# Second feed-forward product and the residual's last token tile with GpSimd at rest

## Chip, cores, metric

One core of one Trainium2 chip runs the whole layer as one program. The metric is the device time of a run in microseconds (us). TensorE multiplies, VectorE and GpSimd do element-wise work, ScalarE copies and activates, SyncE (SP) issues all DMAs.

## What is computed

One layer of a diffusion backbone over 1024 latent tokens of width 1024 with 256 context tokens. Three mixer branches are merged, added to `x`, and followed by a SwiGLU feed-forward with sandwich RMSNorm. What matters here is its end, float32 throughout:

```python
x = x + mod_x[2] * rms_norm(mix, norm_g[l, 1])
h2 = modulate(x, norm_g[l, 2], mod_x[3], mod_x[4])
x = x + mod_x[5] * rms_norm(swiglu(h2, w_ffn_in[l], w_ffn_out[l]), norm_g[l, 3])
# swiglu: gate, up = split(h @ w_in); (silu(gate) * up) @ w_out     D_FF = 2816
```

## The kernel before, in words

**High and low parts.** Each float32 operand of a matmul is cut in two: the high part is a ScalarE copy into the fp32r type, the low part is the operand minus the high part, by VectorE or GpSimd. `parts_product` (L74) issues three matmuls, high by high (L78), high by low (L79) and low by high (L80), of 128x512 each.

**Seven products.** The feed-forward matrices are multiplied with a two-by-two scheme of seven products for eight (Winograd's), P1 to P7. It needs sums and differences of tiles, made by VectorE in SBUF, each of which is cut again.

**residual_ffn_in** (L2012) first makes the output projection of the mixer, one token tile t of 128 rows after the other (0 to `LAST` = 7), adds it to `x`, normalises the rows, turns them on TensorE (L2188) and modulates them into `h2`. Then it runs over 22 pairs of weight tiles (pair p, gate and up), with seven products of 12 matmuls each. Pair 0 begins before the last token tile is done, in the order 0, 3, (0 of pair 1), 1, 2, 4, 6, 5. For it VectorE and GpSimd make the parts of the turned operands while the rows of tile 7 are still on the way:

- VectorE's loop over t ends for t = 7 with the copy of product 0 from PSUM to `t1` (L2614), which product 3 waits for; then it writes `h2` for half the rows, two sums (L2649, L2651), three `part_lower` (L2551), `second_sum` (L2554), the far low parts of T2 (L2661), `fourth_sum` (L2558), the low parts of T4 and `z` (L2680), then the sums for pair 1 (`s13` L2569/L2571, `s2`, `s4`). Product 1 waits for the seventh `part_lo`.
- GpSimd makes sums (L2463, L2466, L2518, L2523, L2527), low parts of weights (`first_weight_lo` L2473 for two tiles of pair 0; `weight_lo` L2477 for later pairs), the near low part of T2 and the four of B22 (`t_part_lo` L2481). Then it makes only `weight_lo` in the loop over the pairs.
- ScalarE makes the high parts (`t1_hi`, `t3_hi`, `t_part_hi`, `weight_hi`), squares and SiLU.

**ffn_out** (L2891) is the second product. It has 7 x 11 = 77 steps s of 12 matmuls each, in the order P1, P5, P6, P3, P2, P7, P4. A step uses one slot of a ring of six with four parts: w high (L2860) and f high (L2862) on ScalarE, w low on VectorE (L2872), f low on GpSimd (`pool_cut`, L2867). VectorE also makes the sum of w tiles for a later product (`dve_sum`, L2886) in steps of P1, P5, P3 and P2. The raw tiles come by DMA (`sp_load`): f into four buffers, w into six, of which P1 and P3 take two a step (`W_LOADS`); a w buffer is free once its sum is made, an f buffer once its low part is (L2841 waits for it). The first steps are started inside the last pair of `residual_ffn_in` by `early[...]`: loads for steps 0 to 4, cuts and sums for steps 0 and 1. The sums of the last activation pair (`keep["last_sums"]`, L2720 to L2724) run in VectorE's step 6, their store (L2154) in SP's step 8.

TensorE waits for banks: `join` (L3036) adds a finished PSUM bank to rows in SBUF, after P3 (before P2 takes the banks), after P2, and after P7 (before P4 goes on in them). Of the first 512 rows, `lower` (VectorE, L3039) scales 128x1024 and GpSimd adds `x` (L3026); the store and the reload of `x` follow (L2921, L2922). The last 512 rows end with L3066, L3073, L3078 and the store L2925.

Each engine runs its own list in order, so the order of calls in a block is its schedule; all waits are semaphores.

Of the kernel before, what the change touches and what calls it, by code (L numbers as in the profile page):

```python
# [41 lines left out]
P = 128  # L42
# [1969 lines left out]
def residual_ffn_in(nc, sem, block, banks, io, keep):  # L2012
# [8 lines left out]
    with ExitStack() as ctx:  # L2021
# [57 lines left out]
        keep["f_stored"] = ((PRODUCT_STEPS - 1, keep["ffn"]["stored"][0]), (PRODUCT_STEPS, keep["ffn"]["stored"][2]),  # L2079
# [31 lines left out]
        def _(sp):  # L2111
# [52 lines left out]
            for p in (FC - 2, FC - 1):  # L2164
                if p == FC - 2:
                    sp.wait_ge(fw_lo_ready, (FC - 1) * PRODUCTS)
                    for s in range(3):
                        early["sp"](sp, s)
                if p == FC - 1:
                    for s in range(3, 5):  # L2170
                        early["sp"](sp, s)
# [101 lines left out]
        def _(act):  # L2273
# [96 lines left out]
            modulate(LAST - 1, 0, 5)  # L2370
            square_x(LAST)
# [78 lines left out]
        def _(pool):  # L2450
# [20 lines left out]
            def first_weight_lo(i):  # L2471
                pool.wait_ge(w0_hi, w0_at(i))
                pool.tensor_tensor(f_lo[i], source(0, i), f_hi[i].bitcast(F32), ALU.subtract).then_inc(w0_lo, 1)  # L2473

# [4 lines left out]
            def t_part_lo(n, ks, at, hi, done):  # L2479
                pool.wait_ge(t_hi_ready[n], hi)  # L2480
                pool.tensor_tensor(t_lo[:, n, ks, at], src[n][:, ks, at], t_hi[:, n, ks, at].bitcast(F32), ALU.subtract)\  # L2481
                    .then_inc(done, 1)

            def step(p, q):
                if q == FC - 1:
                    early["pool"](pool, 0)
                    early["pool"](pool, 1)
# [40 lines left out]
            for i in W0[3:]:  # L2528
                first_weight_lo(i)
            t_part_lo(T2, slice(0, KH), slice(0, HALF // 2), 1, t_lo_ready[T2])  # L2530
            for k in range(KH):
                t_part_lo(B22, k, slice(0, HALF), k // 2 + 1, t_lo_ready[B22])
# [5 lines left out]
        def _(v):  # L2538
# [17 lines left out]
            def fourth_sum(at, count):  # L2556
                v.wait_ge(t2_sum, count)
                v.tensor_tensor(src[T4][:, :, at], src[T4][:, :, at], src[T2][:, :, at], ALU.subtract).then_inc(t4_sum, 1)  # L2558

# [38 lines left out]
            for t in range(TL):  # L2598
# [13 lines left out]
                if t == LAST:  # L2612
                    v.wait_ge(prod0, prod0_at(0))
                    v.tensor_copy(t1, banks[0]).then_inc(t1_ready, 1)  # L2614
# [5 lines left out]
                v.tensor_scalar(xn[:], x[t % 2][:], root(1), None, ALU.mult).then_inc(xn_ready, 1)  # L2620
                if 1 <= t <= FH:
                    h_parts(t - 1)
                if t == LAST - 1:
# [4 lines left out]
                    for i in W0[:3]:  # L2628
                        v.wait_ge(w0_hi, w0_at(i))
                        v.tensor_tensor(f_lo[i], source(0, i), f_hi[i].bitcast(F32), ALU.subtract).then_inc(w0_lo, 1)  # L2630
# [31 lines left out]

# [587 lines left out]
```

## Time and profile before

| | us |
|---|---|
| runs before: median (lowest, highest) of 3 | 1833.17 (1830.52, 1833.98) |
| the profiled execution: its own time | 1832.09 |
| its span, first to last instruction | 1830.0 |
| TensorE busy (matmul) | 1762.9 (96%) |
| VectorE busy | 1236.0 (68%) |
| ScalarE busy | 801.9 (44%) |
| GpSimd busy | 886.6 (48%) |

A matmul's busy time is modelled and overlaps its neighbour's, so the distance between starts tells TensorE's pace, and gaps tell its waits. "Idle before" is time in which the engine stood before an instruction, and the name behind it is what ended the wait. The second product runs from 1596 us to the end, the last token tile of the residual from about 1155 to 1205 us.

### The profile page before, as it was taken

How to read it: one execution, taken by the hardware profiler on the slowest of the kernel's cores; microseconds unless marked ns; L12 is line 12 of the kernel's file. 1: busy time of each engine (PE TensorE's matmuls, PEld its weight loads, DVE VectorE, ACT ScalarE, POOL GpSimd, SP SyncE). 2: the span in 40 equal slices, each digit the busy share in tenths (PEclk: the TensorE clock that was granted, in tenths of full speed). 3: DMA queues.
4: the chain of work that ended last, by engine and by line, in shares of the span. 5: the costliest groups of instructions: out<-in, count | busy, mean ns of one | idle time of the engine just before them, and what ended most of it. 6: DMA issues, size and time to landing. Idle time of an engine off the chain costs nothing.

```text
span 1830.0 us, 25729 instructions
## 1 busy us (share of the span) xinstructions
PE 1762.9 (96%) x9180; PEld 1489.0 (81%) x9180; DVE 1236.0 (68%) x1634; ACT 801.9 (44%) x1579; POOL 886.6 (48%) x550
## 2 busy tenths in 40 slices
PE   8999999999989999899999999899999999989997
PEld 6997888888878888798988878678888888878785
DVE  3528688889949888577743366875565665675866
ACT  3434333335537777555520145543333333344453
POOL 0307677775526967320022242665555555454564
PEclk9999999999999999999999999899999999999998
DMA  8333234336585665411034242123224232376624
GB/s 314 107 106 132 93 149 166 123 138 235 217 204 149 153 159 143 107 32 70 1 138 155 88 161 88 74 93 126 92 103 138 92 126 92 135 264 209 235 89 167
DMA packets 98375, 249.86 MB, mean 137 GB/s; under 512 B 12257, under 2 KB 25953, under 8 KB 98146
## 3 DMA queue, kind: packets, MB, share of 16 engines
q1 hardware_dynamic: 98274, 248.52, 40.7%
q8 instruction: 63, 1.03, 0.2%
q14 instruction: 38, 0.31, 0.1%
HBM read 183.07 MB, written 65.41 MB: 136 GB/s over the span
## 4 chain that ended last, share of the span: by engine, by line
PE 81%; DVE 9%; ACT 3%; DMA 2%; issue 2%; SPq 1%; POOL 1%; PEldq 0%; DVEq 0%; ACTq 0%; POOLq 0%
PE psum L78 19%; PE psum L79 18%; PE psum L80 18%; PE psum L106 3%; PE psum L109 3%; PE psum L107 3%; PE psum L1251 3%; PE psum L1589 2%; PE psum L1238 2%; PE psum L1239 2%; PE psum L1246 1%; PE psum L1575 1%; DVE wmx L1777 1%; DVE mx L1345 1%; PE psum L409 1%
## 5 line engine op out<-in xcount | busy, mean ns | idle before, releaser
L729 POOL TENSOR_TENSOR ring<-raw_w,ring 128x512 fp32r<-128x512 f32 x120 | 187.3, 1579 | 137.5 <-ACT ring L600 137.5
L78 PE MATMUL psum<-h_hi,ring 128*128 128x512 f32 x400 | 155.9, 390 | 3.3 <-ACT z L646 2.0
L79 PE MATMUL psum<-h_lo,ring 128*128 128x512 f32 x400 | 155.6, 389 | 0.0
L80 PE MATMUL psum<-h_hi,ring 128*128 128x512 f32 x400 | 155.6, 389 | 0.0
L78 PE MATMUL psum<-u_slot 128*128 128x512 f32 x308 | 122.4, 398 | 11.8 <-DVE u_high L3036 5.6
L80 PE MATMUL psum<-u_slot 128*128 128x512 f32 x308 | 121.8, 395 | 0.0
L79 PE MATMUL psum<-u_slot 128*128 128x512 f32 x308 | 121.6, 395 | 0.0
L600 ACT ACTIVATE ring<-raw_w 128x512 fp32r<-128x512 f32 x120 | 72.5, 625 | 98.9 <-DVE raw_w L889 31.7
L1286 ACT ACTIVATE e<-psum,neg_m 128x1280 f32<-128x1280 f32 x64 | 85.1, 1330 | 43.5 <-DVE neg_m L1346 43.5
L1345 DVE TENSOR_REDUCE mx<-psum 128x1 f32<-128x1280 f32 x64 | 95.1, 1486 | 5.7 <-PE psum L1239 3.1
L2477 POOL TENSOR_TENSOR cut_lo<-i_raw,cut_hi 128x512 fp32r<-128x512 f32 x44 | 66.8, 1520 | 59.3 <-ACT cut_hi L2331 59.3
L78 PEld LDWEIGHTS psum<-h_hi,ring 128*128 128x128 f32 x400 | 75.1, 188 | 19.9 <-issue 3.4
L2477 POOL TENSOR_TENSOR cut_lo<-stage,cut_hi 128x512 fp32r<-128x512 f32 x40 | 59.9, 1499 | 64.0 <-ACT cut_hi L2331 64.0
L80 PEld LDWEIGHTS psum<-h_hi,ring 128*128 128x128 f32 x400 | 75.1, 188 | 15.8
L79 PEld LDWEIGHTS psum<-h_lo,ring 128*128 128x128 f32 x400 | 75.1, 188 | 15.4
L2867 POOL TENSOR_TENSOR u_slot<-u_f,u_slot 128x512 fp32r<-128x512 f32 x39 | 55.4, 1423 | 59.1 <-ACT u_slot L2862 59.1
L78 PEld LDWEIGHTS psum<-u_slot 128*128 128x128 f32 x308 | 59.0, 192 | 25.9 <-DVE u_slot L2872 7.8
L2867 POOL TENSOR_TENSOR u_slot<-h,u_slot 128x512 fp32r<-128x512 f32 x38 | 55.5, 1466 | 48.5 <-ACT u_slot L2862 48.5
L1251 PE MATMUL psum<-val,at 128*128 128x128 f32 x640 | 76.9, 275 | 1.1 <-ACT at L1293 1.1
L1671 ACT ACTIVATE we<-psum,wneg_m 128x640 f32<-128x640 f32 (+1 forms) x64 | 49.1, 768 | 65.8 <-DVE wneg_m L1779 63.0
L1238 PE MATMUL psum<-k_st,q_st 128*128 128x512 f32 (+1 forms) x192 | 72.4, 384 | 4.9 <-ACT e L1286 3.9
L78 PE MATMUL psum<-m_parts,i_hi 128*128 128x512 f32 x176 | 70.5, 401 | 5.4 <-issue 5.1
(410 smaller groups left out, 5405.7 us busy)
## 6 DMA issues: line engine op xcount, KB each, us to landing
raw_w<-in_w_pairs SPq DMA_DIRECT2D x40, 512.0 KB, 4.8
qk_dram<-room SPq DMA_DIRECT2D x26, 512.0 KB, 3.6
room<-in_w_ada SPq DMA_DIRECT2D x24, 512.0 KB, 4.9
gates_dram<-ost SPq DMA_DIRECT2D x24, 512.0 KB, 3.1
b_g<-gates_dram SPq DMA_DIRECT2D x8, 1536.0 KB, 7.7
stage<-in_w_ff SPq DMA_DIRECT2D x22, 512.0 KB, 5.9
i_raw<-in_w_ff SPq DMA_DIRECT2D x22, 512.0 KB, 5.0
f_dram<-h SPq DMA_DIRECT2D x22, 512.0 KB, 3.1
```

Of the source, the lines that this page charges most:

```text
L78: pe.matmul(out, sh, mh, start=first, stop=False, skip_group_check=onto)
L79: pe.matmul(out, sh, ml, start=False, stop=False, skip_group_check=onto)
L80: return pe.matmul(out, sl, mh, start=False, stop=last, skip_group_check=onto)
L106: pe.matmul(out, sh, mh, start=first, stop=False)
L600: act.activation(w_hi[i], source(p, i), ACT.Copy).then_inc(w_hi_ready, 1)
L729: pool.tensor_tensor(w_lo[i], source(p, i), w_hi[i].bitcast(F32), ALU.subtract).then_inc(w_lo_ready, 1)
L1238: pe.matmul(out, q, k_st[j][:, s, c0:c0 + w], start=True, stop=False)
L1251: mm = pe.matmul(bank[:, 2 * P:3 * P], at[t % 2][:, k, :], val[t // TL % 2][:, k, :], start=(k == 0), stop=(k == TT - 1))
L1286: act.activation(e[i % 2][s][:], psum[:, 3 * s * HALF:3 * s * HALF + TOK], ACT.Exp, scale=SCALE, bias=neg_m[:, i % 2, s:s + 1], accum_out= ...
L1345: ch.link(v.tensor_reduce(mx[:, s:s + 1], psum[:, 3 * s * HALF:3 * s * HALF + TOK], AX.X, ALU.max))
L2477: pool.tensor_tensor(f_lo[i], source(q, i), f_hi[i].bitcast(F32), ALU.subtract).then_inc(fw_lo_ready, 1)
L2867: pool.tensor_tensor(slot[:, 3, :], keep["f_raw"][s % F_RAWS], slot[:, 2, :].bitcast(F32), ALU.subtract).then_inc(b["f_lo_sem"], 1)
```

## The change

- **Second product.** The low part of f moves from GpSimd to VectorE (`f_cut`), as does the last addition to the lower rows (`lower_out`), one `lower` or `lower_out` a step. GpSimd keeps only the f cuts of steps 0 and 1. The second w tile of P1 and P3 gets four buffers of its own (`seconds`), loaded from behind the last products on; the six others hold one main tile a step. Sums come two steps later (`SUM_LAG`), behind the join after P3. The last activation sums move from step 6 to 10, their store from step 8 to 14. The early loads grow to four and then two steps.
- **Residual, last token tile.** `t1` is copied by ScalarE. The low parts of weights 4 and 5 of pair 0, of T2's near half and of B22 move from GpSimd to VectorE; `fourth_sum` goes ahead of T2's low parts.

```diff
@@ -2076,7 +2076,7 @@
-        keep["f_stored"] = ((PRODUCT_STEPS - 1, keep["ffn"]["stored"][0]), (PRODUCT_STEPS, keep["ffn"]["stored"][2]),
+        keep["f_stored"] = ((PRODUCT_STEPS - 1, keep["ffn"]["stored"][0]), (PRODUCT_STEPS, (fs_out, 16 * (FC // 2 - 1))), (2 * PRODUCT_STEPS - 1, keep["ffn"]["stored"][2]),
@@ -2164,10 +2164,10 @@
-                    for s in range(3):
+                    for s in range(F_RAWS):
...
                 if p == FC - 1:
-                    for s in range(3, 5):
+                    for s in range(F_RAWS, F_RAWS + 2):
@@ -2368,6 +2368,9 @@
+            act.wait_ge(prod0, prod0_at(0))
+            act.wait_ge(taken, TL)
+            act.activation(t1, banks[0], ACT.Copy).then_inc(t1_ready, 1)
@@ -2468,23 +2471,14 @@
-            def first_weight_lo(i):
-                pool.wait_ge(w0_hi, w0_at(i))
-                pool.tensor_tensor(f_lo[i], source(0, i), f_hi[i].bitcast(F32), ALU.subtract).then_inc(w0_lo, 1)
...
-            def t_part_lo(n, ks, at, hi, done):
-                pool.wait_ge(t_hi_ready[n], hi)
-                pool.tensor_tensor(t_lo[:, n, ks, at], src[n][:, ks, at], t_hi[:, n, ks, at].bitcast(F32), ALU.subtract)\
-                    .then_inc(done, 1)
...
                 if q == FC - 1:
-                    early["pool"](pool, 0)
-                    early["pool"](pool, 1)
+                    early["f"](pool, 0)
+                    early["f"](pool, 1)
@@ -2525,11 +2519,6 @@
-            for i in W0[3:]:
-                first_weight_lo(i)
-            t_part_lo(T2, slice(0, KH), slice(0, HALF // 2), 1, t_lo_ready[T2])
-            for k in range(KH):
-                t_part_lo(B22, k, slice(0, HALF), k // 2 + 1, t_lo_ready[B22])
@@ -2556,6 +2545,10 @@
+            def first_weight_lo(i):
+                v.wait_ge(w0_hi, w0_at(i))
+                v.tensor_tensor(f_lo[i], source(0, i), f_hi[i].bitcast(F32), ALU.subtract).then_inc(w0_lo, 1)
@@ -2610,14 +2603,15 @@
                 if t == LAST:
-                    v.wait_ge(prod0, prod0_at(0))
-                    v.tensor_copy(t1, banks[0]).then_inc(t1_ready, 1)
+                    first_weight_lo(4)
...
+                if t == LAST:
+                    first_weight_lo(5)
@@ -2626,8 +2620,7 @@
                     for i in W0[:3]:
-                        v.wait_ge(w0_hi, w0_at(i))
-                        v.tensor_tensor(f_lo[i], source(0, i), f_hi[i].bitcast(F32), ALU.subtract).then_inc(w0_lo, 1)
+                        first_weight_lo(i)
@@ -2660,10 +2653,11 @@
+            v.wait_ge(t4_sum, 2)
+            fourth_sum(far, FH - 1)
+            t_part_lo(T2, slice(0, KH), slice(0, HALF // 2), 1, t_lo_ready[T2])
...
-            v.wait_ge(t4_sum, 2)
-            fourth_sum(far, FH - 1)
@@ -2728,10 +2722,8 @@
-                    early["sum"](v, 0)
...
-                    early["sum"](v, 1)
@@ -2750,6 +2742,8 @@
+            for k in range(KH):
+                t_part_lo(B22, k, slice(0, HALF), k // 2 + 1, t_lo_ready[B22])
@@ -2765,27 +2759,29 @@
-RING, F_RAWS, W_RAWS = 6, 4, 6
+RING, F_RAWS, W_RAWS, SECONDS = 6, 4, 6, 4
...
-W_LOADS = {P1: (("even", 0), ("even", 1)), P5: (("odd", 1),), P3: (("odd", 1), ("even", 1)), P2: (("odd", 0),)}
+W_MAIN = {P1: ("even", 0), P5: ("odd", 1), P3: ("odd", 1), P2: ("odd", 0)}
+W_SECOND = {P1: ("even", 1), P3: ("even", 1)}
...
-def loads_until(s):
+SUM_LAG = 2
+def load_of(table, s):
...
-    return sum(len(W_LOADS.get(n, ())) for n in range(i)) * PRODUCT_STEPS + j * len(W_LOADS.get(i, ()))
+    return sum(n in table for n in range(i)) * PRODUCT_STEPS + j
+def step_of(table, n):
+    return sorted(table)[n // PRODUCT_STEPS] * PRODUCT_STEPS + n % PRODUCT_STEPS
...
-def step_of_load(n):
-    return next(s for s in range(STEPS) if loads_until(s) <= n < loads_until(s + 1))
@@ -2802,10 +2798,11 @@
+        seconds = [sb(f"u_second{n}", [P, HALF])[:] for n in range(SECONDS)]
...
-    stage, w_in = keep["stage"], keep["u_in"]
+    stage, w_in, second_in = keep["stage"], keep["u_in"], [sem(f"fo_second{n}") for n in range(SECONDS)]
@@ -2820,19 +2817,32 @@
-        return other[:, j, :] if i == P7 else chain[j] if i in SUMS_OF else w_raw[loads_until(s) % W_RAWS]
-    def landed(eng, n):
+        return other[:, j, :] if i == P7 else chain[j] if i in SUMS_OF else w_raw[load_of(W_MAIN, s) % W_RAWS]
+    def landed(eng, s):
+        n = load_of(W_MAIN, s)
...
+    def rows_of(s, what):
+        rows, half = what
+        chunk = 2 * (s % PRODUCT_STEPS) + (rows == "odd")
+        return io["w_ffn_out"][chunk * P:(chunk + 1) * P, half * HALF:(half + 1) * HALF]
+    def sp_second(sp, s):
+        if s // PRODUCT_STEPS not in W_SECOND:
+            return
+        n = load_of(W_SECOND, s)
+        if n >= SECONDS:
+            sp.wait_ge(b["w_sum_sem"], sums_until(step_of(W_SECOND, n - SECONDS)))
+        sp.dma_start(seconds[n % SECONDS], rows_of(s, W_SECOND[s // PRODUCT_STEPS])).then_inc(second_in[n % SECONDS], 16)
...
-        for a, (rows, half) in enumerate(W_LOADS.get(i, ())):
-            n, chunk = loads_until(s) + a, 2 * j + (rows == "odd")
+        if i in W_MAIN:
+            n = load_of(W_MAIN, s)
             if n >= W_RAWS:
-                sp.wait_ge(b["w_sum_sem"], sums_until(step_of_load(n - W_RAWS)))
-            sp.dma_start(w_raw[n % W_RAWS], io["w_ffn_out"][chunk * P:(chunk + 1) * P, half * HALF:(half + 1) * HALF])\
-              .then_inc(w_in[n % W_RAWS], 16)
+                sp.wait_ge(b["w_sum_sem"], sums_until(step_of(W_MAIN, n - W_RAWS)))
+            sp.dma_start(w_raw[n % W_RAWS], rows_of(s, W_MAIN[i])).then_inc(w_in[n % W_RAWS], 16)
@@ -2854,17 +2864,17 @@
-            landed(act, loads_until(s))
+            landed(act, s)
...
-    def pool_cut(pool, s):
+    def f_cut(eng, s):
...
-        pool.wait_ge(b["f_hi_sem"], s + 1)
-        pool.tensor_tensor(slot[:, 3, :], keep["f_raw"][s % F_RAWS], slot[:, 2, :].bitcast(F32), ALU.subtract).then_inc(b["f_lo_sem"], 1)
+        eng.wait_ge(b["f_hi_sem"], s + 1)
+        eng.tensor_tensor(slot[:, 3, :], keep["f_raw"][s % F_RAWS], slot[:, 2, :].bitcast(F32), ALU.subtract).then_inc(b["f_lo_sem"], 1)
@@ -2875,17 +2885,19 @@
-        n = loads_until(s)
-        raws = [w_raw[(n + a) % W_RAWS] for a in range(len(W_LOADS[i]))]
-        for a in range(len(raws)):
-            landed(v, n + a)
+        landed(v, s)
+        main, second = w_raw[load_of(W_MAIN, s) % W_RAWS], None
+        if i in W_SECOND:
+            n = load_of(W_SECOND, s)
+            v.wait_ge(second_in[n % SECONDS], 16 * (n // SECONDS + 1))
+            second = seconds[n % SECONDS]
...
-        out, left, right = {P1: lambda: (chain[j], raws[1], raws[0]), P5: lambda: (chain[j], raws[0], chain[j]),
-                            P3: lambda: (other[:, j, :], raws[0], raws[1]), P2: lambda: (chain[j], raws[0], chain[j])}[i]()
+        out, left, right = {P1: (chain[j], second, main), P5: (chain[j], main, chain[j]),
+                            P3: (other[:, j, :], main, second), P2: (chain[j], main, chain[j])}[i]
...
-    keep["ffn_out"], keep["ffn_out_cuts"] = b, {"sp": sp_load, "act": act_cut, "pool": pool_cut, "dve": dve_cut, "sum": dve_sum}
+    keep["ffn_out"], keep["ffn_out_cuts"] = b, {"sp": sp_load, "act": act_cut, "f": f_cut, "dve": dve_cut, "sum": dve_sum, "second": sp_second}
@@ -2907,12 +2919,15 @@
     def _(sp):
-        for s in range(5, STEPS):
+        sp.wait_ge(*before["products"])
+        for s in range(SECONDS):
+            cuts["second"](sp, s)
+        for s in range(6, STEPS):
+            cuts["second"](sp, s - SUM_LAG)
...
-            if s == 8:
+            if s == 14:
...
             if s == 3 * PRODUCT_STEPS:
-                sp.wait_ge(*before["products"])
@@ -3015,16 +3030,6 @@
-    @block.gpsimd
-    def _(pool):
-        for s in range(2, STEPS):
-            cuts["pool"](pool, s)
-            t = s - (end_of(P2) + RING + 6)
-            if 0 <= t < T:
-                pool.wait_ge(y_ready, t + 1)
-                pool.wait_ge(x_in[t], 16)
-                nc.gpsimd.tensor_tensor(low[:, t, :], low[:, t, :], x[t][:], ALU.add).then_inc(out_ready, 1)
@@ -3039,13 +3044,22 @@
+        def lower_out(t):
+            v.wait_ge(y_ready, t + 1)
+            v.wait_ge(x_in[t], 16)
+            v.tensor_tensor(low[:, t, :], low[:, t, :], x[t][:], ALU.add).then_inc(out_ready, 1)
+        LOWER = {5: (lower, 0), 6: (lower_out, 0), 7: (lower, 1), 8: (lower_out, 1), 9: (lower, 2), 11: (lower_out, 2),
+                 12: (lower, 3), 13: (lower_out, 3)}
+        v.wait_ge(b["f_lo_sem"], 2)
...
-            cuts["sum"](v, s)
-            if s == 6:
-                keep["last_sums"]()
+            cuts["f"](v, s)
             if s == end_of(P3) + RING - 1:
                 join(P3, Y, low, right)
+            cuts["sum"](v, s - SUM_LAG)
+            if s == 10:
+                keep["last_sums"]()
@@ -3055,8 +3069,9 @@
-            if 0 <= s - (end_of(P2) + RING + 5) < 4:
-                lower(s - (end_of(P2) + RING + 5))
+            if s - end_of(P2) - RING in LOWER:
+                finish, t = LOWER[s - end_of(P2) - RING]
+                finish(t)
```

## Rows read from the trace of the kernel before

**Rows 1.** Waits of TensorE, 1560 to 1831 us: total, times, longest.

```profile
PE psum L78 <- DVE u_high L3036: 5.6, 1, 5.6
PE psum L78 <- POOL u_slot L2867: 3.7, 1, 3.7
PE psum L78 <- DVE u_slot L2872: 1.4, 1, 1.4
PE psum L78 <- DVE u_low L3036: 1.2, 1, 1.2
```

**Rows 2.** Tile u_slot: ns min/median/max, first and last start.

```profile
L78 PE MATMUL psum<-u_slot x308: 387/389/766, 1596.2 to 1823.1; 128*128 128x512 f32 x154
...
L2872 DVE TENSOR_TENSOR u_slot<-stage,u_slot x22: 675/692/1757, 1586.2 to 1735.0; 128x512 fp32r<-128x512 f32 x22
```

**Rows 3.** Timeline of TensorE: start, duration, what; quiet stretch.

```profile
1639.66 0.39 PE L80 MATMUL psum<-u_slot 128*128 128x512 f32 x1
...
1719.94 0.39 PE L79 MATMUL psum<-u_slot 128*128 128x512 f32 x1
```

**Rows 4.** Busy by stretch: length, PE, PEld, DVE, ACT, POOL, granted clock, DMA.

```profile
1620.00:1630.00 10.00, 6.32 (x21) 4.80 (x20) 5.66 (x6) 5.34 (x9) 4.40 (x3) 0.75 0.96 341
```

**Rows 5.** Chain that ended last: start, us, what.

```profile
1627.03 0.43 PE psum L79
```

**Rows 6.** Timelines of VectorE and GpSimd in the second product.

```profile
1597.93 1.79 DVE L2708 TENSOR_TENSOR h<-i_g,i_z 128x512 f32<-128x512 f32 x1
...
1723.29 1.78 DVE L2886 TENSOR_TENSOR u_chain<-u_first,u_chain 128x512 f32<-128x512 f32 x1
...
1784.28 2.31 DVE L3039 SCALAR_TENSOR_TENSOR u_low<-u_low,u_ss,late_row 128x1024 f32<-128x1024 f32 x1
...
1723.24 1.28 POOL L2867 TENSOR_TENSOR u_slot<-u_f,u_slot 128x512 fp32r<-128x512 f32 x1 [1.44 <-ACT u_slot L2862]
```

**Rows 7.** Tile u_high: ns min/median/max, first and last start.

```profile
L2982 ACT ACTIVATE u_high<-psum x4: 578/591/604, 1665.7 to 1667.2; 128x512 f32<-128x512 f32 x4
L3036 DVE TENSOR_TENSOR u_high<-psum,u_high x4: 673/674/677, 1790.9 to 1792.7; 128x512 f32<-128x512 f32 x4
...
L3078 DVE SCALAR_TENSOR_TENSOR u_high<-u_high,u_ss,u_x x4: 1284/1286/1286, 1817.5 to 1825.7; 128x1024 f32<-128x1024 f32 x4
```

**Rows 8.** Timeline of SP, the DMA issues.

```profile
1615.14 0.55 SPq L2154 DMA_DIRECT2D fs_dram<-h  x1
1615.73 1.69 SPq L2834 DMA_DIRECT2D stage<-in_w_ffn_out  x2
```

**Rows 9.** DMA issues of 1598 to 1603 us: size, median us to landing.

```profile
u_first<-in_w_ffn_out SPq DMA_DIRECT2D x2, 256.0 KB, 3.0
```

**Rows 10.** DMA issues of 1585 to 1640 us.

```profile
stage<-in_w_ffn_out SPq DMA_DIRECT2D x17, 256.0 KB, 5.1
```

**Rows 11.** Timeline of TensorE at the last token tile: [idle before <- releaser].

```profile
1162.70 0.50 PE L78 MATMUL psum<-b_hi,cut_hi 128*128 128x512 f32 x1 [2.96 <-DVE gate_row L2614]
...
1176.54 0.77 PE L78 MATMUL psum<-m_parts,i_hi 128*128 128x512 f32 x1 [5.09 <-issue]
```

**Rows 12.** Timelines at the last token tile: ScalarE, GpSimd, VectorE.

```profile
1159.41 1.83 ACT L2298 ACTIVATE h<-psum,B,A 128x128 f32<-128x128 f32 x5
...
1172.50 2.79 POOL L2481 TENSOR_TENSOR i_t_lo<-h,i_t_hi 128x1024 fp32r<-128x1024 f32 x1
...
1169.78 1.64 DVE L2649 TENSOR_TENSOR h<-h 128x512 f32<-128x512 f32 x1 [0.17 <-ACT h L2298]
...
1173.01 4.03 DVE L2551 TENSOR_TENSOR m_parts<-h,m_parts 128x512 fp32r<-128x512 f32 x3
1176.96 1.21 DVE L2554 TENSOR_TENSOR h<-h 128x1024 f32<-128x1024 f32 x1
...
1187.93 1.77 DVE L2569 TENSOR_TENSOR i_s<-i_raw 128x512 f32<-128x512 f32 x1
...
1205.41 0.69 DVE L2680 TENSOR_TENSOR i_z<-i_z,psum 128x512 f32<-128x512 f32 x1 [1.33 <-ACT i_z L2393]
```

## Prediction

> **What bounds the kernel now.** I read the waits of TensorE first. In the last 270 us it stops four times, for 1.4, 3.7, 1.2 and 5.6 us, 11.9 us in all, each time for a low part or a join on VectorE or GpSimd [rows 1]. The rest of the second feed-forward product is TensorE alone. Its 308 first matmuls start from 1596.2 to 1823.1 us [rows 2]. The undisturbed pitch comes from a quiet stretch: 354 matmuls start from 1639.66 to 1719.94 us, so 80.28 / 353 = 0.2274 us each [rows 3]. A step is 12 matmuls, 2.73 us, and 307 groups of three would take 209.4 us; they take 226.9. The stage loses 17.5 us. 11.9 are the four waits. The other 5.6 come from the clock: after the 3.7 us stop the granted clock of the slice is 0.75, between its two levels of 1.2 and 2.4 GHz [rows 4], and the matmuls stand 0.43 us apart [rows 5]. The first restart has 12 such pitches and the second 8, which is 20 x 0.20 = 4.0 us, and 1.6 us go into the uneven first matmuls after the four stops.
>
> Why is VectorE late, when its low part takes 0.69 us at the median [rows 2]? The timeline shows it. At 1723.24 GpSimd begins a 1.28 us cut, at 1723.29 VectorE a sum, and the sum ends 0.55 us after GpSimd: 1.78 us instead of 0.69 [rows 6]. A 128x1024 product of three operands in SBUF takes 2.31 us beside GpSimd [rows 6] and 1.29 us without it [rows 7]. So the two engines take turns on such operands. That, and not the amount of work, makes the four stops.
>
> **Start of the product.** Before, the weights of a step share six buffers, two for each step of the first eleven, so the queue waits for VectorE's sums, which stand behind the last activation product. The load behind the 3.7 us stop was issued at 1615.73, right behind the store of sums at 1615.14 that had waited for VectorE [rows 8]. After: a main tile for each of six steps and four f tiles are loaded early, the sums come two steps later, the store moves from step 8 to step 14. Everything that VectorE does in a step is then low part of w, low part of f, sum: 3 x 0.69 = 2.07 us [rows 2] against 2.73 us. GpSimd's 75 cuts of this block are gone. So the first two stops (1.4, 3.7) and the first slow clock stretch vanish, if nothing else is late.
>
> What is late next is the new second tile. Its load stands behind the wait for the last products (over by 1596.2) and the f store, which waits for VectorE's last product. That took 1.79 us from 1597.93 beside GpSimd [rows 6] and would take 0.69, so 1598.6. Issue of the store, 0.55 us as at 1615.14 [rows 8], puts the second tile's at 1599.2. VectorE makes the parts of step 2 by 1600.0 and then stands at the sum of step 0, with the parts of step 3, the next sum and all f loads from step 6 on behind it. TensorE wants step 3 at 1596.2 + 3 x 2.73 = 1604.4. The nearest landing, of the loads issued just here before, is 3.0 us [rows 9]: 1602.2. Sum, w part, f part: 2.07 us, 1604.3. Loss about 0. The far row is the 5.1 us median of the crowded stretch [rows 10]: 1604.3 + 2.07 = 1606.4, loss 2.0 us. I take 0.3, since one 512 KB store is ahead, as it was for the loads of [rows 9]. The Trainium skill (DMA: Bandwidth & Descriptors, Anatomy of one DMA) gives a fixed 2.0 us plus bytes over 436 GB/s; as an estimate, 2.6 us for 256 KB, by which the loss would be 0. The trace lies above it, at 3.0 and 5.1.
>
> Behind that, VectorE's 2.07 us a step lets it gain on TensorE. The loads are the same in number and size as before, only earlier; I cost them at nothing. What hides them is VectorE's lead of up to five steps (the ring); without it each would cost what it lands late, at most the 5.1 us of [rows 10].
>
> **Joins and residual rows.** The join of P3 now comes before the sum. In the old order the sum of 1.78 us stood ahead of it [rows 6]; now a 0.69 us f part does. The w part ends as the sum began, at 1723.3, the f part by 1724.0, the first join of 0.67 us [rows 7] by 1724.7. Before, it ended at 1723.29 + 1.78 + 0.67 = 1725.7, and TensorE had waited 1.2, so it wants the bank at 1724.5. The 1.2 us stop shrinks to 0.2. The rows' two passes over `low` (2.31 us on VectorE, more on GpSimd) cost VectorE now 1.29 + 1.29 us a tile, one pass a step: 2 x 0.69 + 1.29 = 2.67 us, still under 2.73, with the six-slot ring (five steps, 13.6 us) as cover. So the join of P7 should not be late: 5.6 us become 0.2, and the second clock stretch goes. If the cover were gone, what remains is 4 x 1.29 us.
>
> Sum for this block: 17.5 lost before, 0.3 + 0.2 + 0.2 after and 0.3 for restarts: 1.0. **Gain 16.5 us.** Bounds: 14 (the far landing, half a restart) and 17.5.
>
> **The residual's last tile.** TensorE's large waits here are 3.0 us for the copy of t1 and 5.1 us, shown as issue [rows 11]. The copy moves to ScalarE, which is free at 1161.24 [rows 12] and needs 0.59 us [rows 7]: TensorE goes on at 1161.9, not 1162.7 [rows 11]. That is not kept. VectorE's low part 4 takes the copy's place, meets GpSimd and delays the row mean by up to 0.5 us. With it go xn, ScalarE's next parts and GpSimd's first low part of the next pair, for which TensorE waits next. I take 0.3 us later there, between 0 and 0.6.
>
> The 5.1 us stop that ends at 1176.5 is VectorE's chain: two sums of 1.64 us and three parts in 4.03 us, beside GpSimd's low parts, of which one runs 2.79 us from 1172.50 [rows 12]. With GpSimd done by about 1170, that is one op of about 1.3 and four of 0.69: 4.1 us instead of 7.3, and the seventh part, the one TensorE needs, ends at 1172.8 rather than 1176.5. TensorE itself is ready at 1171.5 (1176.54 - 5.09), so the stop shrinks to 1.3.
>
> Then VectorE has more to do: the near T2 part (1.29), four B22 parts (4 x 0.69) which were GpSimd's. The chain ran 1176.96 to 1187.93 before its first sum for the next pair, with ScalarE and TensorE between. I walk it: second sum 1174.5, fourth sum 1175.9, T2 parts 1178.5, T4 and z by 1181.8, B22 by 1184.4. The next pair's first sum took 1.77 us at 1187.93 beside GpSimd [rows 12], 0.69 when alone, 1.1 us more. Gain 3.5 + 1.1 = 4.6 us. From here the chain is VectorE's to the z of pair 1 at 1205.41 [rows 12], after which TensorE waits no more, so what VectorE gains there is kept; slow clock saved at 1177 is absorbed in this chain. **Gain 4.6 us**, bounds 1.5 (rival C) and 7 (also the slow clock).
>
> **Sum.** 16.5 + 4.6 = 21.1 us off the profiled 1832.1 is 1811.0. The median of the runs is 1.1 us above the profiled one: 1812.1. I give 1812.
>
> **Rivals.**
> A, slower: the turn-taking is not what stretches VectorE; its ops stay at the means they have in this block. Low parts are then about 0.98 us and sums 1.2. Against 0.91 (a third of 2.73), the point from which it decides, a step with a sum takes 3.16 us: 44 such steps x 0.43 = 19 us lost, with the two join stops (6.8) and 3 us of clock kept: 1812 + 29 = 1841. For it: VectorE takes 75 cuts and 4 row passes more. Against: pairs as at 1723 [rows 6], and a 0.69 median [rows 2]. 4%. The Trainium skill (SBUF — State Buffer, SBUF: two separate sides) has one exclusive pair of ports for the two engines, held for a whole instruction; the trace agrees, with 0.55 us behind the end of GpSimd's cut [rows 6].
> B: the second tile lands late, 6.7 us or so. TensorE stops 3.6 us at step 3 and gets half clock as it did at 1626 (2.7 us): 1818. For it: VectorE is in order and everything stands behind the sum. Against: the queue is empty but for one store. 12%.
> C: the residual's gain is lost, because VectorE has 5 us more work in a chain that was its own: only the 1.1 us and a little remain, 1815. 14%.
> D: VectorE's row passes and the squares' wait reach into the P7 join; half of the stop and a clock stretch stay: 1816 to 1818. 6%.
> E: the change does not do what it says, since GpSimd keeps the sums and weight parts of the residual and the pairs and is at rest only in the last block: the residual gives nothing, 1816. 3%, for the block itself keeps its gain.
>
> **Numbers.** Forecast 61%, A 4, B 12, C 14, D 6, E 3. The bounds of the terms give 1808 to 1817; with B, C, D and E the range is 1808 to 1820, which leaves out A and little else. A measurement can tell 0.2%, 3.7 us, from no change: faster 94%, same 2%, slower 4%.
>
> **What would show it.** No GpSimd work after the first two cuts; VectorE's u_slot and u_chain ops all at 0.69 us; TensorE's waits in the last block together under 1.5 us and granted clock 1.00 in all its full slices; ScalarE, not VectorE, writing t1; the stop at 1176 near 1.3 us and starting product 1 at about 1173; the second product's first to last matmul in about 210.5 us. The forecast is wrong if a stop over 2 us with half clock stands near step 3, if a join is waited for, or if the residual chain to the z of pair 1 ends less than 3 us earlier.

## The result, and the profile after

| | before | after |
|---|---|---|
| runs: median (lowest, highest), us | 1831.92 (1830.52, 1833.98) of 4 | 1812.52 (1808.0, 1820.69) of 4 |
| ratio, 95% interval | | 0.9885 [0.9856, 0.9913] |
| the profiled execution, us | 1832.09 | 1820.69 |
| its span, us | 1830.0 | 1818.9 |

The change saves 1.15%, 19.4 us between the medians; the forecast was 1812.0, in a range of 1808 to 1820. A second series of five rounds gave a ratio of 0.9879 [0.9852, 0.9906] (`after_again`, below); in it one run of the kernel before, in a slow state, took 3553.69 us and is left out of the medians.

The two profiled executions are only 11.4 us apart. The missing part lies ahead of the changed code, where both kernels are the same. Here is the busy time by stretch of the attention stage, columns as in [rows 4]; first the kernel after:

```profile
720.00:760.00 40.00, 35.58 (x236) 31.70 (x235) 20.94 (x35) 22.49 (x56) 20.97 (x17) 0.89 0.37 118
760.00:800.00 40.00, 38.81 (x254) 36.36 (x255) 22.90 (x71) 20.38 (x47) 11.05 (x6) 0.86 0.31 71
```

and the kernel before:

```profile
720.00:760.00 40.00, 35.58 (x270) 31.70 (x269) 22.32 (x43) 22.69 (x56) 20.97 (x17) 1.00 0.40 127
760.00:800.00 40.00, 38.34 (x291) 35.55 (x290) 28.27 (x85) 23.89 (x56) 13.35 (x8) 1.00 0.29 66
```

In 80 us the kernel after makes 71 matmuls fewer (236 + 254 against 270 + 291) at a granted clock of 0.89 and 0.86: an episode in which the clock is partly at its lower level. Kernels that are the same up to here had it in some executions and not in others: `block_only` and `gpsimd_keeps_f` (both 0.89 in the second of these slices) did, `rest_only` and `t_parts_gpsimd` (1.00 in both) did not. So I measure stages, not totals. The last matmul ahead of the stop for `t1` starts at 1159.35 before and at 1169.63 after, 10.28 us later. From there:

| stretch, us | before | after | gain |
|---|---|---|---|
| residual: last matmul ahead of the `t1` stop, to the restart behind `z` of pair 1 | 1159.35 to 1206.24: 46.89 | 1169.63 to 1210.84: 41.21 | 5.7 |
| from there to the first matmul of the second product | 389.96 | 389.96 | 0.0 |
| second product, first to last start of the 308 | 1596.2 to 1823.1: 226.9 | 1600.8 to 1812.1: 211.3 | 15.6 |
| last of the 308 to the end of the span | 6.9 | 6.8 | 0.1 |

5.7 + 15.6 + 0.1 = 21.4 us, less the 10.3 of the episode is 11.1, the difference of the spans.

**Second product.** The engines' busy time from the page, GpSimd's by slice, and all waits of TensorE from 1560 to 1820 us in the kernel after:

```profile
PE 1765.8 (97%) x9180; PEld 1493.8 (82%) x9180; DVE 1228.2 (68%) x1719; ACT 801.0 (44%) x1580; POOL 754.2 (41%) x464
...
POOL 0307677775525967330012232445555555400000
```

```profile
PE psum L78 <- DVE u_slot L2877: 0.7, 1, 0.7
```

GpSimd is silent in the last five slices. Of the four waits of [rows 1], 11.9 us together, one of 0.7 is left. VectorE has 86 instructions of GpSimd's more across the program (550 - 464), and yet is busy for 8 us less than the 1236.0 of before. The tile u_slot and the windows say why:

```profile
L2877 DVE TENSOR_TENSOR u_slot<-h,u_slot x38: 680/684/693, 1603.6 to 1795.0; 128x512 fp32r<-128x512 f32 x38
...
L2882 DVE TENSOR_TENSOR u_slot<-u_first,u_slot x23: 680/692/694, 1610.2 to 1777.7; 128x512 fp32r<-128x512 f32 x23
L2882 DVE TENSOR_TENSOR u_slot<-stage,u_slot x22: 681/692/693, 1590.8 to 1736.8; 128x512 fp32r<-128x512 f32 x22
```

```profile
1600.00:1640.00 40.00, 39.27 (x173) 32.11 (x172) 31.65 (x51) 18.26 (x33) 0.00 (x0) 1.00 0.82 282
...
1760.00:1800.00 40.00, 39.91 (x176) 32.66 (x175) 32.53 (x48) 22.29 (x42) 0.00 (x0) 1.00 0.46 158
```

VectorE's slowest cut is 694 ns, where [rows 2] had 1757, and the clock is 1.00 where [rows 4] had 0.75. The wait that is left comes from the second w tile (`u_second`). It shows in the timelines of SP and VectorE and the DMA issues of 1600 to 1610 us:

```profile
1603.12 0.55 SPq L2173 DMA_DIRECT2D f_dram<-h  x1
1603.70 5.17 SPq L2837 DMA_DIRECT2D u_second<-in_w_ffn_out  x5
...
1607.82 0.69 DVE L2898 TENSOR_TENSOR u_first<-u_second,stage 128x512 f32<-128x512 f32 x1 [3.53 <-issue]
1608.43 0.69 DVE L2882 TENSOR_TENSOR u_slot<-stage,u_slot 128x512 fp32r<-128x512 f32 x1
1609.03 0.68 DVE L2877 TENSOR_TENSOR u_slot<-h,u_slot 128x512 fp32r<-128x512 f32 x1
```

```profile
u_second<-in_w_ffn_out SPq DMA_DIRECT2D x5, 256.0 KB, 4.1
```

Issued at 1603.70, landed by 1607.82, and the low part of f, third from there, ends at 1609.71: TensorE goes on at 1609.87. In the kernel before, the first loads of [rows 9] were issued farther behind the same store, 2.53 us and not 0.58:

```profile
1599.74 0.55 SPq L2173 DMA_DIRECT2D f_dram<-h  x1
1602.27 0.80 SPq L2834 DMA_DIRECT2D u_first<-in_w_ffn_out  x2
```

**Residual.** TensorE's timeline at the last token tile (to compare with [rows 11], take off 10.28):

```profile
1169.63 0.39 PE L80 MATMUL psum<-b_hi,cut_lo 128*128 128x512 f32 x1
1172.07 0.50 PE L78 MATMUL psum<-b_hi,cut_hi 128*128 128x512 f32 x1 [2.05 <-ACT gate_row L2373]
...
1179.21 0.50 PE L78 MATMUL psum<-b_hi,cut_hi 128*128 128x512 f32 x1 [2.30 <-POOL cut_lo L2476]
...
1182.99 0.47 PE L78 MATMUL psum<-m_parts,i_hi 128*128 128x512 f32 x1 [0.72 <-issue]
...
1210.84 0.47 PE L78 MATMUL psum<-i_t_hi,cut_hi 128*128 128x512 f32 x1 [1.30 <-POOL i_lo L2476]
```

The 5.09 us stop is 0.72. Before, six matmuls from 1164.59 and ten from 1177.11 stood 0.43 us apart, at a granted clock of 0.50, behind the stops of 2.96 and 5.09; now none does. What TensorE gains by that in the first of the two stretches it gives up in a wait: the one that ends at 1179.21 is 2.30 us and was 0.22. The timelines of VectorE and GpSimd:

```profile
1172.26 1.78 DVE L2551 TENSOR_TENSOR cut_lo<-stage,cut_hi 128x512 fp32r<-128x512 f32 x1
...
1183.40 1.22 DVE L2543 TENSOR_TENSOR h<-h 128x1024 f32<-128x1024 f32 x1
1184.73 1.23 DVE L2547 TENSOR_TENSOR h<-h 128x1024 f32<-128x1024 f32 x1
1185.87 3.63 DVE L2654 TENSOR_TENSOR i_t_lo<-h,i_t_hi 128x1024 fp32r<-128x1024 f32 x5
1189.41 0.68 DVE L2674 TENSOR_TENSOR i_z<-i_z,psum 128x512 f32<-128x512 f32 x1
1190.01 3.69 DVE L2654 TENSOR_TENSOR i_t_lo<-h,i_t_hi 128x512 fp32r<-128x512 f32 x6
1193.62 0.69 DVE L2562 TENSOR_TENSOR i_s<-i_raw 128x512 f32<-128x512 f32 x1
...
1195.78 1.29 POOL L2476 TENSOR_TENSOR i_lo<-i_raw,i_hi 128x512 fp32r<-128x512 f32 x1 [15.38 <-ACT i_hi L2331]
```

GpSimd is idle for 15.38 us, and VectorE goes through ten low parts of 128x512 and one of 128x1024 in 7.3 us. It starts the first sum of pair 1 at 1193.62. Counted from the last matmul ahead of the stop, as all stages here, that is 1183.34 on the clock of before, 4.6 us ahead of its 1187.93, and the sum takes 0.69 rather than 1.77 [rows 12].

### The profile page after: what moved, and what is told of

It reads as the page before. It is cut to its first block and busy times, and to the rows that moved or that the text cites. A ratio compares the mean times of both kernels' runs of the same rounds, so it can differ in the third digit from the quotient of the medians.

```text
span 1818.9 us, 25732 instructions
## 1 busy us (share of the span) xinstructions
PE 1765.8 (97%) x9180; PEld 1493.8 (82%) x9180; DVE 1228.2 (68%) x1719; ACT 801.0 (44%) x1580; POOL 754.2 (41%) x464
## 5 line engine op out<-in xcount | busy, mean ns | idle before, releaser
L78 PE MATMUL psum<-u_slot 128*128 128x512 f32 x308 | 120.4, 391 | 0.9 <-DVE u_slot L2877 0.7
L80 PE MATMUL psum<-u_slot 128*128 128x512 f32 x308 | 120.1, 390 | 0.0
L79 PE MATMUL psum<-u_slot 128*128 128x512 f32 x308 | 119.9, 389 | 0.0
L78 PEld LDWEIGHTS psum<-h_hi,ring 128*128 128x128 f32 x400 | 75.1, 188 | 19.4 <-issue 3.4
L79 PEld LDWEIGHTS psum<-h_lo,ring 128*128 128x128 f32 x400 | 75.1, 188 | 15.3
L1251 PEld LDWEIGHTS psum<-val,at 128*128 128x128 f32 x640 | 75.9, 196 | 1.8 <-ACT at L1293 1.0
L78 PE MATMUL psum<-b_hi,cut_hi 128*128 128x512 f32 x176 | 69.0, 392 | 5.1 <-POOL cut_lo L2476 2.3
L78 PE MATMUL psum<-i_t_hi,cut_hi 128*128 128x512 f32 x176 | 68.6, 390 | 1.3 <-POOL i_lo L2476 1.3
```

Of the source, the lines that this page charges most:

```text
L78: pe.matmul(out, sh, mh, start=first, stop=False, skip_group_check=onto)
L79: pe.matmul(out, sh, ml, start=False, stop=False, skip_group_check=onto)
L80: return pe.matmul(out, sl, mh, start=False, stop=last, skip_group_check=onto)
L1251: mm = pe.matmul(bank[:, 2 * P:3 * P], at[t % 2][:, k, :], val[t // TL % 2][:, k, :], start=(k == 0), stop=(k == TT - 1))
```

## The experiments

The theory: VectorE and GpSimd take turns on operands in SBUF, and GpSimd's rest, not the new buffers, gives most of the gain. Each run is read by the two stage times, residual (46.9 before, 41.2 after) and second product (226.9 and 211.3), from one profiled execution each.

**One part alone.** `block_only` keeps `residual_ffn_in`'s last tile as it was, and `residual_only` keeps the second product as it was:

```diff
 # block_only
-            act.activation(t1, banks[0], ACT.Copy).then_inc(t1_ready, 1)
+            for i in W0[3:]:
+                first_weight_lo(i)          # on GpSimd, and t_part_lo of T2 and B22 too
 # residual_only
-RING, F_RAWS, W_RAWS, SECONDS = 6, 4, 6, 4
+RING, F_RAWS, W_RAWS = 6, 4, 6
```

> The change in the second product alone, the residual's last tile as before. If the two parts are separate, as the working has it, the first to last of the 308 first matmuls of the second product take 211.3 us as in the changed kernel (226.9 before), TensorE waits 3.0 and 5.1 us again at the last tile, and the time is 15.6 us below before. If part of the block's gain hung on the earlier arrival from the residual, the block would take 213 us or more.

> The change at the residual's last tile alone, the second product as before. Separate parts: the block takes 226.9 us, and from TensorE's last matmul before the t1 wait to its restart behind the z of pair 1 there are 41.2 us instead of 46.9, so 5.7 us below before. If the residual's gain is only a loan that later pairs take back, the second product starts less than 3 us earlier.

Measured: `block_only` 46.97 and 211.6, `residual_only` 41.22 and 226.5. The two parts add without touching each other: 15.3 and 5.7 us.

**GpSimd's rest alone.** The second product with the buffers, loads, sums and stores of before, but `pool_cut` and the lower rows' addition called from VectorE's list, and the join of P3 where it was. The passes over the lower rows are spread one a step, as in the changed kernel:

```diff
         for s in range(2, STEPS):
             cuts["dve"](v, s)
+            cuts["pool"](v, s)
             cuts["sum"](v, s)
```

> Second product: VectorE makes the f low parts and the last additions, GpSimd rests; but loads, buffers, the place of the sums and of the store stay as before, residual as before. Turn-taking theory: all VectorE ops are at 0.69 us, the first two stops all but vanish because the sums and the store come earlier by themselves, the P3 join waits under 1 us since the sum of 0.69 us is ahead of it, the P7 join not at all: block 210.5 to 213 us. Load-order theory (the gain is from the new buffers, the later sums and the later store): the 3.7 us stop and its clock stretch stay, block 217 us or more.

**GpSimd not at rest.** The changed kernel, with the f cuts and the addition left on GpSimd, and VectorE's four passes in four steps in a row, as before:

```diff
+    @block.gpsimd
+    def _(pool):
+        for s in range(2, STEPS):
+            cuts["f"](pool, s)
...
-            cuts["f"](v, s)
```

> The changed kernel with new buffers, load order, late sums and store, but the f low parts from step 2 on and the last additions on GpSimd. Turn-taking theory: VectorE's ops that meet GpSimd take 1.6 to 1.8 us again, the passes over the lower rows 2.3; the P7 join waits 3 us or more with half clock behind it, block 217 to 222 us. Load-order theory: the block is within 1 us of the changed kernel's 211.3.

Measured: second product 212.7 in `rest_only` (1598.1 to 1810.8) and 220.8 in `gpsimd_keeps_f` (1598.2 to 1819.0). The waits of TensorE in `rest_only`:

```profile
PE psum L78 <- DVE u_slot L2867: 1.5, 1, 1.5
PE psum L78 <- DVE u_low L3026: 0.7, 1, 0.7
```

and in `gpsimd_keeps_f`, with VectorE's and GpSimd's timelines around the long one:

```profile
PE psum L78 <- DVE u_high L3051: 5.6, 1, 5.6
PE psum L78 <- DVE u_slot L2882: 1.7, 2, 1.3
```

```profile
1774.22 2.32 DVE L3054 SCALAR_TENSOR_TENSOR u_low<-u_low,u_ss,late_row 128x1024 f32<-128x1024 f32 x1
1776.46 2.88 DVE L2882 TENSOR_TENSOR u_slot<-u_first,u_slot 128x512 fp32r<-128x512 f32 x1
...
1785.92 2.47 DVE L3051 TENSOR_TENSOR u_high<-psum,u_high 128x512 f32<-128x512 f32 x4
...
1785.41 2.81 POOL L3041 TENSOR_TENSOR u_low<-u_low,u_x 128x1024 f32<-128x1024 f32 x1
```

With the arrangement of before, the rest alone gives 14.2 of the 15.6 us, in spite of 79 instructions more on VectorE. The spread of the passes is in these 14.2; no run has the one without the other. The new arrangement without the rest gives 6.1 (226.9 - 220.8): the 3.7 us stop and the wait at the join of P3 are gone and two short waits of 1.7 us together are left, but the join of P7 waits 5.6 us as in [rows 1]. There VectorE's 0.69 us cut takes 2.88 and its 1.29 us pass 2.32, beside GpSimd's cuts and additions. The join itself, four operations with one operand in PSUM, is not stretched, though it runs beside an addition of GpSimd's: it takes 2.47 us, one operation every 0.60 us. On top of the rest the arrangement is worth 1.4.

**Is it the turn-taking, or the work?** Two kernels give GpSimd work whose result nobody reads, beside the changed kernel's second product. `extra_tt` adds 75 subtractions of 128x512 from SBUF, `extra_memset` 150 fills of 128x512:

```diff
+        for s in range(2, STEPS):
+            pool.wait_ge(b["f_hi_sem"], s + 1)
...
+            pool.tensor_tensor(b["extra"], spare[:, 0:HALF], spare[:, HALF:D], ALU.subtract)   # extra_tt
+            pool.memset(b["extra"], 0.0)                                        # extra_memset, twice
```

> The changed kernel, and beside each step of the second product one GpSimd subtraction of 128x512 float32 from SBUF whose result nobody reads; VectorE's work is as in the changed kernel. Turn-taking theory: VectorE's three ops a step meet it, those met take 1.3 to 1.8 us, a summed step costs VectorE about 2.07 + 1.1 = 3.2 us against 2.73, so the block grows from 211.3 to 225 us or more. If GpSimd only did harm through results that came late, the block stays at 211.3 since nobody waits for it.

> The same with two GpSimd fills of 128x512 with zero a step, which read nothing from SBUF. If any GpSimd access takes the turn, VectorE's ops stretch as in the run with subtractions. If only a GpSimd op that reads SBUF does, they stay at 0.69 us and the block at 211.3. The Trainium skill (SBUF — State Buffer, SBUF: two separate sides) says the second for VectorE ops with two SBUF inputs.

Measured: residual 41.2 in both, second product 244.6 with the subtractions and 211.3 with the fills. The 308 first matmuls and the busy time by stretch, `extra_tt`:

```profile
L78 PE MATMUL psum<-u_slot x308: 387/389/765, 1591.1 to 1835.7; 128*128 128x512 f32 x154
...
1600.00:1640.00 40.00, 34.63 (x144) 27.97 (x145) 39.93 (x47) 17.87 (x31) 21.47 (x12) 0.96 0.79 262
```

`extra_memset`:

```profile
L78 PE MATMUL psum<-u_slot x308: 389/389/473, 1588.0 to 1799.3; 128*128 128x512 f32 x154
L2883 DVE TENSOR_TENSOR u_slot<-stage,u_slot x22: 684/693/696, 1578.0 to 1724.1; 128x512 fp32r<-128x512 f32 x22
...
1600.00:1640.00 40.00, 40.00 (x178) 32.98 (x177) 35.77 (x58) 22.79 (x40) 18.29 (x35) 1.00 0.87 296
```

GpSimd is busy for 21.5 and 18.3 of 40 us, much the same, but VectorE makes 47 instructions in 39.9 us of busy time in the one and 58 in 35.8 in the other. Timelines of `extra_tt`:

```profile
1719.37 1.77 DVE L2899 TENSOR_TENSOR u_other<-stage,u_second 128x512 f32<-128x512 f32 x1
...
1718.88 1.71 POOL L3042 TENSOR_TENSOR u_extra<-gate_row 128x512 f32<-128x512 f32 x1 [0.58 <-ACT u_slot L2873]
1720.95 1.31 POOL L3042 TENSOR_TENSOR u_extra<-gate_row 128x512 f32<-128x512 f32 x1 [0.36 <-ACT u_slot L2873]
```

The sum of 1719.37 meets an operation of 1718.88 that ends at 1720.59, and ends itself at 1721.14, 0.55 us later, the distance of [rows 6]. Nothing of VectorE's waits for the extra work or shares its tile, so what is left to join the two is the way to the operands in SBUF. With nothing read, the longest of VectorE's cuts in this block is 696 ns. The Trainium skill (SBUF — State Buffer, section SBUF: two separate sides) says that a VectorE operation with two SBUF inputs contends only against a GpSimd operation that reads SBUF. These two runs agree: 33 us with reads, nothing with fills.

**The residual, taken apart.** `t_parts_gpsimd` gives T2's near part and the four of B22 back to GpSimd. `t1_vectore` gives the copy of t1 back to VectorE:

```diff
 # t_parts_gpsimd, in GpSimd's list
+            t_part_lo(T2, slice(0, KH), slice(0, HALF // 2), 1, t_lo_ready[T2])
+            for k in range(KH):
+                t_part_lo(B22, k, slice(0, HALF), k // 2 + 1, t_lo_ready[B22])
 # t1_vectore, in VectorE's list
                 if t == LAST:
+                    v.wait_ge(prod0, prod0_at(0))
+                    v.tensor_copy(t1, banks[0]).then_inc(t1_ready, 1)
                     first_weight_lo(4)
```

> The changed kernel with the near T2 and the four B22 low parts back on GpSimd; t1 on ScalarE and weights 4 and 5 on VectorE stay. VectorE has 4 us less work in its chain, but meets GpSimd. Turn-taking theory: T2's 2.7 us part on GpSimd starts by 1180 of the changed kernel's clock and stretches the sums and parts beside it, the z of pair 1 comes 1 to 4 us later than in the changed kernel. Work theory: VectorE's shorter list lets it come 2 us or more earlier.

> The changed kernel with the copy of t1 back on VectorE, ahead of the low part of weight 4. Theory (the chain of the last token tile is VectorE's own work; its copy was 0.6 us of it): the stretch from the last matmul ahead of t1 to the restart behind z of pair 1 grows from 41.2 to about 41.8 us, the stop for t1 goes from 2.05 us to about 2.9. Rival, the prediction's step: the copy's move is not kept, as TensorE's next waits end with other work; then 41.2 stays. The block of the second product stays at 211.3 us in both.

Measured: residual 45.28 in `t_parts_gpsimd` and 41.20 in `t1_vectore`, with the second product at 211.3 and 211.2. In `t_parts_gpsimd`, TensorE, GpSimd and VectorE:

```profile
1174.64 0.76 PE L78 MATMUL psum<-m_parts,i_hi 128*128 128x512 f32 x1 [2.82 <-issue]
...
1169.97 2.81 POOL L2480 TENSOR_TENSOR i_t_lo<-h,i_t_hi 128x1024 fp32r<-128x1024 f32 x1
...
1170.59 2.75 DVE L2652 TENSOR_TENSOR h<-h 128x512 f32<-128x512 f32 x1
```

One part of GpSimd's holds a 0.69 us sum until 0.56 us behind its own end, and the stop is 2.8 instead of 0.7. So 4.1 of the 5.7 us come from these five parts, a little more than the 1 to 4 expected. If the parts add, the other 1.6 belong to the low parts of weights 4 and 5 and to the order of the sums, which I did not part. VectorE in `t1_vectore`:

```profile
1163.88 0.68 DVE L2604 COPY gate_row<-psum 128x512 f32<-128x512 f32 x1
1164.48 1.16 DVE L2548 TENSOR_TENSOR cut_lo<-stage,cut_hi 128x512 fp32r<-128x512 f32 x1
...
1166.17 1.17 DVE L2611 TENSOR_SCALAR o_xn<-o_x,o_rs 128x1024 f32<-128x1024 f32 x1
```

My expectation of 0.6 us more was a miss. The copy takes 0.60 from start to start, but the cut behind it then starts later against GpSimd's operation and takes 1.16 instead of 1.78. `xn` starts 4.91 us behind the last matmul ahead of the stop, 4.95 in the changed kernel (1174.58 - 1169.63). The `t1` stop is longer (2.97 for 2.05), the wait that ended at 1179.21 in the changed kernel is shorter (0.71 for 2.30), and nothing of the copy's move is kept.

**Can more be had?** `better` loads the four second tiles ahead of the last f store (behind the wait for the last products, inside SP's last pair), makes both joins before the f cut of their step, and puts the low parts of weights 4 and 5 both behind `xn`. `joins_seconds` does the same without the last:

```diff
+                    sp.wait_ge(prod_done, FC * PRODUCTS)
+                    for s in range(SECONDS):
+                        early["second"](sp, s)
...
-            cuts["f"](v, s)
             if s == end_of(P3) + RING - 1:
                 join(P3, Y, low, right)
+            if s == end_of(P7) + RING - 1:
+                join(P7, X, high, right)
+            cuts["f"](v, s)
```

> The changed kernel with three edits: the four second tiles are loaded ahead of the last f store (behind the wait for the products), both late weight low parts come behind the normalised rows at the last tile, and both joins come ahead of the f low part. Expected: VectorE's 3.5 us wait at the sum of step 0 falls under 1.5 and TensorE's 0.7 us stop at step 3 goes (1.1 us with the restart), the row mean of the last tile comes 0.5 us earlier with 0.5 us in the z of pair 1, and the two joins' 0.25 us each go: 2 us in all, block 210 us.

> The changed kernel, unaltered, beside the kernel before in five rounds. Theory (the change gives back 5.7 us in the residual and 15.6 in the second product): 21.3 us less than the kernel before, a ratio of 0.9884. Rival (the 11.4 us between the profiled executions is the change's worth, and the difference of the earlier stages belongs to it): 0.9938. By stage: residual 41.2, second product 211.3.

> The changed kernel with the four second tiles loaded ahead of the last store of activations, and both joins ahead of the low part of f of their step; the residual as in the changed kernel. Theory (the late second tile costs 0.8 us, the two joins 0.25 each, with restarts 1.7 in all): second product 209.6 us, no stop over 0.3 us in it, residual 41.2, so 1.7 us less than the changed kernel in the same rounds, a ratio to the kernel before of 0.9875. Rival (something else ends those waits, VectorE's lead of the first steps): the second product stays above 210.8.

Measured: `better` residual 41.52, second product 209.6. The block came out as hoped. The residual became 0.3 us slower and not 0.5 faster, a miss: `xn` starts 0.4 us earlier, 4.54 us behind the last matmul ahead of the stop, but with both cuts behind it the next low part (L2543) starts 0.9 us later, at 7.87 instead of 6.96. That part is dropped in `joins_seconds`: residual 41.30, second product 209.5. Against the kernel before, on the same chip and in the same rounds (median 1833.80 of the eight other runs):

| | median (lowest, highest), us | ratio, 95% interval |
|---|---|---|
| `after_again` | 1812.17 (1811.68, 1820.63) of 6 | 0.9879 [0.9852, 0.9906] |
| `joins_seconds` | 1809.65 (1808.77, 1811.31) of 5 | 0.9864 [0.9837, 0.9892] |

`after_again` has 41.24 and 211.3 in its profile, as the changed kernel. The 1833.80 - 1812.17 = 21.6 us fit the 21.4 of the stages and not the 11.4 between the profiled executions: the interval holds the theory's 0.9884 and leaves out the rival's 0.9938. `joins_seconds` is faster than the changed kernel by 2.5 us of median: its slowest run is below the fastest of `after_again`, and 1.7 of it is seen in the stages (1.8 less 0.1). Tile u_slot, SP and VectorE in `joins_seconds`:

```profile
L78 PE MATMUL psum<-u_slot x308: 389/389/401, 1591.5 to 1801.0; 128*128 128x512 f32 x154
```

```profile
1591.65 1.75 SPq L2840 DMA_DIRECT2D u_second<-in_w_ffn_out  x4
1593.77 0.55 SPq L2176 DMA_DIRECT2D f_dram<-h  x1
...
1594.87 0.68 DVE L2901 TENSOR_TENSOR u_first<-u_second,stage 128x512 f32<-128x512 f32 x1
```

The sum of step 0 no longer waits, none of the 308 first matmuls takes over 401 ns, and 209.5 us is the 209.4 that the prediction worked out from the quiet pitch [rows 3]: TensorE stops nowhere in this block any more.

## Why the prediction was right, point by point

The total (21.1 us forecast, 21.4 measured by stages) is closer than its terms, whose errors of 0.9 too much and 1.1 too little cancelled: that is luck. So is part of the hit of 1812 on 1812.52. The medians of that series are 19.4 us apart; the forecast started from 1833.17, and the median before over all four runs is 1831.92.

- **What bounds the kernel: right.** 209.4 us as the block's floor was met by `joins_seconds` (209.5). That the two engines' turns make the stops is shown by `extra_tt` and `extra_memset`; that the turns and not the late loads are the main cause, by `rest_only`.
- **Second product: 16.5 forecast, 15.6 measured, inside the bounds (14 to 17.5).** The mis-sized term is the loss at step 3, taken as 0.3 and in truth 0.9 with its restart. The walk held at each point, 4.6 us later than on the clock of before: store at 1603.12 (forecast 1598.6 + 4.6 = 1603.2), second tile issued at 1603.70 (1603.8), TensorE ready for step 3 at 1609.0 (1609.0). Only the landing was off: 4.1 us, where I took the 3.0 of [rows 9] and not the 5.1 of [rows 10]. "One store ahead, as it was for those loads" was the reason, and the two cases are not alike. Before, the load was issued 2.53 us behind the store, here 0.58 us. In `joins_seconds` four such loads go out in a row ahead of the store, and VectorE reads the first 3.22 us behind its issue without a wait. That speaks for the store as the cause of the 4.1, and against the loads behind the first; no run parts them cleanly. The Trainium skill (DMA: Bandwidth & Descriptors, Anatomy of one DMA) gives its formula for DMAs that GpSimd issues, while these are issued by SyncE; the estimate from it, 2.6 us, lies farther off still. Each join opens a gap of 0.25 us (forecast 0.2), with no loss of clock. Floor 209.5 + 0.9 + 0.5 leaves 0.4 for the uneven pitch behind the gaps (forecast 0.3).
- **Residual: 4.6 forecast, 5.7 measured, inside 1.5 to 7.** The copy's step was right twice: TensorE went on at 1161.8 on the clock of before (forecast 1161.9), the cut in its place met GpSimd (1.78), the next wait ended at 1168.9 on that clock, 0.5 later than before (0.3 forecast, up to 0.6), and `t1_vectore` shows that nothing of it is kept. Product 1 began at 1172.7 (forecast 1172.8). The stop was 0.7, not 1.3, because TensorE came 0.5 us later to it. The mis-sized term is the walk from there: second and fourth sum ended at 1174.3 and 1175.7 (forecast 1174.5 and 1175.9), but the parts of T2 and T4 and `z` took until 1181.0 and not 1181.8, and B22 until 1183.4 and not 1184.4. T2, T4 and `z` are one part of 128x1024, six of 128x512 and `z`: 1.29 + 7 x 0.69 = 6.1 us by durations, and the walk gave them 5.9. But a run of such operations stands 0.60 to 0.61 us apart from start to start, not 0.69, and the eight took 5.3. So VectorE was 4.6 us ahead behind B22 where 3.5 were forecast, and the 1.1 for the next sum came as said.
- **Rivals.** A (the turns are not the cause) is excluded by the 694 ns. Its price was of the right size: `extra_tt`, where the turns keep VectorE busy for 39.93 of 40 us, shows what a VectorE that can't follow TensorE costs, 33 us against the 29 worked out for A. B (late second tile) came in part, 0.7 us of stop and no half clock. C is excluded by 5.7 us, D by the 0.25 us at the joins, E by GpSimd's 15.38 us of rest in the residual.
- **Left open.** How the last 1.6 us of the residual divide between the weights' low parts and the order of the sums; what the spread of the row passes gives without GpSimd's rest; and what makes the clock episodes.

## What to carry to other kernels

Do not cost work that is moved off GpSimd by its duration on VectorE alone: where both read SBUF, what VectorE gets back from the turns can exceed what it takes on (here, in `rest_only`, 79 instructions more on VectorE and a block 14 us shorter). Before new buffers and a new order are built against a late load, try the plain move first; it gave 14.2 of 15.6 us. And compare stages between two landmarks that both traces share, for an episode in untouched code can hide half of a gain.

## What the runs showed of the hardware

- The same code ahead of the change took 1156.9 us to the last matmul ahead of the `t1` stop in `extra_memset` and 1169.6 in the kernel after. The two slices from 720 to 800 us have a granted clock of 1.00 in the one, 0.89 and 0.86 in the other. Between the two profiles compared here the difference is 10.3 us, as much as half the change.
- Fills by GpSimd cost VectorE nothing, subtractions of the same tile size hold it until 0.55 us behind their end where the two meet, and grow longer themselves: 1.71 us for the one of 1718.88, which starts while a low part of VectorE's runs (1718.77, 0.68), and 1.31 for the one of 1720.95, which starts as a sum ends. GpSimd's busy share, 18 and 21 of 40 us, does not tell the two cases apart.
- VectorE's operations with one operand in PSUM are not held: the four operations of a join take 2.47 us together beside GpSimd's addition of 128x1024 in `gpsimd_keeps_f`, where cuts with both operands in SBUF take 2.88 each instead of 0.69.
- VectorE's subtractions of 128x512 are recorded at 0.68 to 0.69 us, and a run of them starts one every 0.60 to 0.61 us. Costed by duration, such a run comes out 13% too long.
